# A hybrid decoder step on one core: rows spread by TensorE, attention work reordered, small work of the routing moved ahead of the weight splits

## The chip, the cores and the metric

One core of a Trainium2 chip runs the whole step in one launch. The metric is the device time of one execution in microseconds. TensorE (PE) multiplies, VectorE (DVE) and ScalarE (ACT) do elementwise work, GpSimd (POOL) small vector work and some DMA issues, SyncE (SP) issues the loads. TensorE runs at one of two clock levels, 1.2 or 2.4 GHz, and the profile shows which was granted (0.50 or 1.00).

## The reference, cut to what matters

336 tokens (8 sequences of 8 new tokens, 16 meta tokens and 256 prompt tokens; three tiles of 112 rows), D = 1024, go through two layers:

```
layer 0: x += pool(rmsnorm(x, g_mix)) ; pool: per 256-channel group, trailing mean minus token, @ pool_w[g], * pool_scale
         x += swiglu(rmsnorm(x, g_ffn))                                  # dense, D_FF = 2816
layer 1: proj = rmsnorm(x) @ w_in (1024 x 672) -> query latent 384, key/value latent 256, rotary key 32
         q = rmsnorm(cq) @ w_uq ; 16 heads of 64 + 32
         q_lat = q_nope @ w_uk ; scores = q_lat . ckv + q_pe . kpe ; softmax ; (p @ ckv) @ w_uv ; @ w_o
         prompt: 272 keys ; each sample sequence: 1024 cached keys + its own 8 new ones
         x += sum over the top 2 of 8 experts of gate * swiglu(rmsnorm(x))
y = rmsnorm(x)
```

All is float32. The kernel multiplies most of it as pairs of float32r parts: w = wh + wl, x = xh + xl, and three products.

## The kernel before

Each engine runs its own instruction list, joined by semaphores; the order within a list is written out by hand, and an engine never passes an instruction that waits.

**Head.** SP loads the tokens x, the gain g_mix and the scale of the pooling weights; both rows are broadcast by DMA, to 112 and 128 partitions (0.45 and 0.5 MB of writes). Per tile ACT squares (L740), POOL takes the inverse root (L629, L631), DVE multiplies (`norm`, L1054), ACT makes the high half (`tokens_split`, L753) and DVE the low half (L1081). ACT's list squares tile 1 before it makes the high half of tile 0. TensorE pools by multiplying with band matrices (L1590), with products of zeros in between (`add_zeros`, L1578; 40 at the start, 8 after a tile). POOL scales the pooling weights in two halves (L650), ACT and DVE split them (L763, L1092), and 72 matmuls make the pooling output (`three`, L1570 to L1572). DVE adds it, norms, and the dense loop starts at 52.36 us.

**Projection.** `project_in` makes the 672 columns in blocks of 512 and 160 with 24 matmuls each.

**Attention.** After the heads' queries are turned (L1756), TensorE makes all six blocks of values (L1768), then the queries absorbed into the latent space (L1778), then turns the cached keys of the first sequence (`turn_cache`, L1802), and waits for all six copies of these before the first prompt scores (`prompt_scores`, L1818 to L1823). The prompt loop is a pipeline over 20 units (4 groups of one `tail` and four `head` units): scores of u, turn of u-2 (`prompt_turn`, L1831), values of u-3 (`prompt_values`, L1840 to L1852). Then the eight sequences, one after another: scores against the cache (n = 0, 1) and the 8 new keys (n = 2: six matmuls and one for the rotary part), softmax, values (L1941), with the turns for the next sequence and pieces of the output projection (`fill`) in between. SP loads the pages of sequence b+3 once the output of sequence b is made (`load_cache`, one register load and two DMAs per page); POOL copies the rotary keys (L677) before TensorE may turn that sequence.

**Routing.** Three router tiles (L1964), a chain of small DVE operations, counts by TensorE (L1981, L1991), then POOL gathers the first item's tokens by an indirect DMA (L695), TensorE turns them (L1998), ACT and DVE split them, and the expert loop begins: 8 items of 33 weight units (1 MB each, ring of 11), each split by ACT (L732) and DVE (L1066) and used by 12 or more matmuls. The gate weights (`pick`, an Exp on ACT, L995) are made between the first splits. The first Silu (L983) and the first Exp (L919) each have a table load in front.

## Time and profile before

Three runs took 1425.63, 1427.50 and 1430.47 us (median 1427.5). The profiled execution took 1426.08 us, its span is 1424.5 us.

| stretch, us from the start | what | PE busy | granted clock |
|---|---|---|---|
| 0 to 52.4 | head: pooling layer | with gaps | 0.50 from 13.7 to 24.0 and 30.8 to 37.6, else 1.00 |
| 52.4 to 312.3 | dense SwiGLU | full | 1.00 but for 3.4 us |
| 312.3 to 358.9 | projections | 46.16 of 46.60 | 1.00 |
| 376.6 to 406.6 | values, absorbed queries, first turns | with gaps | 0.50 from 392.6 |
| 406.6 to 463.1 | prompt attention | nearly full | 0.50 to 423.3 and twice 3.4 us, else 1.00 |
| 463.1 to 591.3 | eight sequences | 125.6 of 128.3 | 1.00 |
| 591.3 to 639.9 | last projection, routing | with gaps | 0.50 from 617.9 |
| 639.9 to 1424.5 | experts | full but for 1.6 us at 666 and the end | 0.50 to 645.2 and from 669.1 to 672.5, else 1.00 nearly to the end |

How to read it: PE carries 86% of the chain that ended last. An instruction's line gives its start, its duration and, in brackets, how long its engine was idle before it and for whom it waited. PE durations overlap, so a matmul's pace is the distance between starts. SPq rows are DMA issues of SP.

### The profile page before, as it was taken

The numbers are of one execution on the slowest core, as the hardware profiler recorded it, in microseconds if no ns is written. First come the engines' busy times: TensorE is split into PE (matmuls) and PEld (weight loads), VectorE is DVE, ScalarE is ACT, GpSimd is POOL, SyncE is SP. The second block draws the span as 40 slices with busy tenths as digits, with TensorE's granted clock in tenths as the row PEclk, the third lists the DMA queues.
The fourth block names the chain that finished last, engine by engine and source line by source line (L and its number), as shares of the span: only waits on it lengthen the run. The fifth ranks groups of instructions, "written<-read, shape, count | busy, mean of one in ns | idle before, by whom it ended". The sixth has DMA issues, their size and how long they took to land.

```text
span 1424.5 us, 19477 instructions
## 1 busy us (share of the span) xinstructions
PE 1364.4 (96%) x6975; PEld 1122.2 (79%) x6975; DVE 955.5 (67%) x921; ACT 795.2 (56%) x786; POOL 96.7 (7%) x129
## 2 busy tenths in 40 slices
PE   7999999989989999959999999999999999999996
PEld 6899989877667777537888888888888888888884
DVE  4634344355345444347888888888888888888885
ACT  4423333334445333225777777777777777777773
POOL 3000000002200000110001001000010010100100
PEclk7999999999959999968999999999999999999998
DMA  9644443230210422377999999999999999999981
GB/s 265 222 152 135 130 147 118 84 132 12 64 40 1 157 70 59 137 308 270 367 362 365 401 364 369 388 361 390 369 366 400 364 369 387 362 389 370 362 322 37
DMA packets 137428, 355.04 MB, mean 249 GB/s; under 512 B 18426, under 2 KB 54858, under 8 KB 137377
## 3 DMA queue, kind: packets, MB, share of 16 engines
q1 hardware_dynamic: 133769, 342.37, 65.9%
q0 software_dynamic: 3616, 12.09, 2.9%
q8 instruction: 28, 0.46, 0.1%
q14 instruction: 15, 0.12, 0.0%
HBM read 345.38 MB, written 9.20 MB: 249 GB/s over the span
## 4 chain that ended last, share of the span: by engine, by line
PE 86%; SPq 4%; DVE 3%; issue 2%; ACT 2%; DMA 1%; POOL 0%; ACTq 0%; DVEq 0%; POOLq 0%
PE PS L1570 24%; PE PS L1572 24%; PE PS L1571 24%; PE PS L1872 2%; PE PS L2005 1%; SPq L556 1%; SPq L554 1%; SPq L552 1%; PE PS L1941 1%; PE PS L1768 1%; PE PS L1852 1%; DMA X<-in_x_prompt 1%; PE PS L1778 1%; PE PS L1998 1%; PE PS L1590 1%
## 5 line engine op out<-in xcount | busy, mean ns | idle before, releaser
L1066 DVE TENSOR_TENSOR LOW<-RAW,UH 128x2048 fp32r<-128x2048 f32 x275 | 628.3, 2292 | 152.4 <-ACT UH L732 152.4
L732 ACT CAST UH<-RAW 128x2048 fp32r<-128x2048 f32 x275 | 526.2, 1914 | 252.3 <-PE PS L1572 252.2
L1570 PE MATMUL PS<-UH,XH 128*128 128x512 f32 (+1 forms) x768 | 292.1, 380 | 1.4 <-DVE XL L1446 1.4
L1572 PE MATMUL PS<-UH,XL 128*128 128x512 f32 (+1 forms) x768 | 290.2, 378 | 0.0
L1571 PE MATMUL PS<-LOW,XH 128*128 128x512 f32 (+1 forms) x768 | 290.2, 378 | 0.0
L1570 PEld LDWEIGHTS PS<-UH,XH 128*128 128x128 f32 x768 | 145.7, 190 | 30.1 <-DVE XL L1446 1.8
L1572 PEld LDWEIGHTS PS<-UH,XL 128*128 128x128 f32 x768 | 145.3, 189 | 28.8
L1571 PEld LDWEIGHTS PS<-LOW,XH 128*128 128x128 f32 x768 | 145.5, 189 | 28.2
L1570 PE MATMUL PS<-UH,ATH 128*128 128x512 f32 x352 | 138.7, 394 | 1.9 <-DVE ATL L1462 1.9
L1572 PE MATMUL PS<-UH,ATL 128*128 128x512 f32 x352 | 137.9, 392 | 0.0
L1571 PE MATMUL PS<-LOW,ATH 128*128 128x512 f32 x352 | 137.7, 391 | 0.0
L1570 PE MATMUL PS<-HTH,UH 128*128 128x336 f32 x352 | 111.2, 316 | 0.6 <-DVE HTL L1073 0.6
L1571 PE MATMUL PS<-HTL,UH 128*128 128x336 f32 x352 | 110.9, 315 | 0.0
L1572 PE MATMUL PS<-HTH,LOWPAIR 128*128 128x336 f32 x352 | 110.8, 315 | 0.0
L1570 PEld LDWEIGHTS PS<-UH,ATH 128*128 128x128 f32 x352 | 66.5, 189 | 16.1 <-issue 2.3
L1572 PEld LDWEIGHTS PS<-UH,ATL 128*128 128x128 f32 x352 | 66.4, 189 | 14.1
L1571 PEld LDWEIGHTS PS<-LOW,ATH 128*128 128x128 f32 x352 | 66.5, 189 | 13.7
L1066 DVE TENSOR_TENSOR LOWPAIR<-PAIR,UH 128x2048 fp32r<-128x2048 f32 x22 | 50.4, 2293 | 27.9 <-ACT UH L732 27.9
L1570 PEld LDWEIGHTS PS<-HTH,UH 128*128 128x128 f32 x352 | 66.1, 188 | 1.5 <-issue 1.0
L1571 PEld LDWEIGHTS PS<-HTL,UH 128*128 128x128 f32 x352 | 66.2, 188 | 0.4
L1572 PEld LDWEIGHTS PS<-HTH,LOWPAIR 128*128 128x128 f32 x352 | 66.1, 188 | 0.0
L799 ACT CAST AH<-AF 128x336 fp32r<-128x336 f32 x22 | 10.4, 473 | 81.7 <-DVE AF L1144 81.7
(315 smaller groups left out, 1697.0 us busy)
## 6 DMA issues: line engine op xcount, KB each, us to landing
RAW<-in_moe_w_down SPq DMA_DIRECT2D x88, 1024.0 KB, 5.1
RAW<-in_moe_w_gate SPq DMA_DIRECT2D x64, 1024.0 KB, 5.1
RAW<-in_moe_w_up SPq DMA_DIRECT2D x64, 1024.0 KB, 5.0
RAW<-in_moe_w_gate SPq DMA_DIRECT2D x24, 768.0 KB, 7.3
RAW<-in_moe_w_up SPq DMA_DIRECT2D x24, 768.0 KB, 7.6
PAIR<-in_ffn_w_gate SPq DMA_DIRECT2D x11, 1024.0 KB, 5.3
PAIR<-in_ffn_w_up SPq DMA_DIRECT2D x11, 1024.0 KB, 7.8
RAW<-in_ffn_w_down SPq DMA_DIRECT2D x11, 1024.0 KB, 4.9
```

The lines of the kernel that those rows point to most:

```text
L552: page = sp.value_load(PAGES[0:1, b * NPG:(b + 1) * NPG][:, bass.ds(i, 1)], min_val=0, max_val=nphys - 1)
L554: sp.dma_start(CC[b % 3][:, to, 0:KL], a["cache_ckv"][0, one, :, :].rearrange("e p c -> p e c"))\
L556: sp.dma_start(CC[b % 3][:, to, KL:KL + ROPE], a["cache_kpe"][0, one, :, :].rearrange("e p c -> p e c"))\
L732: nc.scalar.copy(dst, src).then_inc(unit_high, 1)
L1066: V_.tensor_tensor(dst, src, high.bitcast(F32), ALU.subtract).then_inc(unit_low, 1)
L1570: mm(out, wh, xh, start=start, stop=False, skip_group_check=True)
L1571: mm(out, wh, xl, start=False, stop=False, skip_group_check=True)
L1572: return mm(out, wl, xh, start=False, stop=stop, skip_group_check=True)
L1590: return mm(PS[:, d, t * TT:t * TT + wide], part[:, t, d * P:(d + 1) * P], pm[min(t, 1)][:, d // 2, 0:wide], start=False, stop=False, skip ...
L1768: ins = mm(PS[0:rows, half, :], CKT[:, c, SMP + p0:SMP + p0 + rows], WUV[:, c, half * 512:(half + 1) * 512], start=(c == 0), stop=(c == 1))
L1778: ins = mm(PS[:, 2 + n, hh * SMP:(hh + 1) * SMP], UKT[:, h, c * P:(c + 1) * P], QTR[0:NOPE, h, 0:SMP], start=True, stop=True)
L1872: ins = mm(PS[0:TT, mix_bank(i), :], OT[:, k, t * TT:(t + 1) * TT], WO[:, k, half * 512:(half + 1) * 512], start=(k == 0), stop=(k == KD - 1))
```

## The change

Nothing of the computed result changes. Head: the two rows are loaded to one partition and multiplied by a row of ones; ACT copies g_mix and DVE pool_scale out of PSUM ahead of the rest. The number of zero products in front goes from 40 to 24, and ten wider ones stand before the pooling output. ACT's tile order changes, one half of the pooling weights is scaled by DVE, an output DMA goes later. The projection's blocks become 336 + 336. Absorbed queries and values alternate, values 4 and 5 go later, all sequences' new-key scores are made once at prompt unit 2, and the wait for the first sequence's turned keys moves behind the first scores. Exp and Silu get a small early use on ACT. In the routing `pick` and the Exp move ahead of splits, `keep_clock` adds 18 and 28 transposes whose output nobody reads, and the first Silu moves ahead of a split.

```diff
+        sp.dma_start(ROWS[:, 0, :], a["g_mix"][0:1, :]).then_inc(rows_in, 16)
+        sp.dma_start(ROWS[:, 1, :], a["pool_scale"][0:1, :]).then_inc(rows_in, 16)
-        sp.dma_start(G[0][:, :], a["g_mix"][0:1, :].partition_broadcast(TT)).then_inc(gain0_in, 16)
-        sp.dma_start(PSC[:, :], a["pool_scale"][0:1, :].partition_broadcast(P)).then_inc(pool_w_in, 16)
...
# POOL
-        pool.dma_start(o["pool_sample"][0, :, 0:BUF - NS, :], a["state_pool"][0, :, NS:BUF, :])...
-        for half in range(2):
+        pool.wait_ge(spread_out, 4)
+        weights, scale = scaled_half(1)
+        pool.wait_ge(pool_w_scaled, 1)
             nc.gpsimd.tensor_tensor(weights, weights, scale, ALU.mult).then_inc(pool_w_scaled, 1)
         pool.wait_ge(normed, NT)
...
+        pool.dma_start(o["pool_sample"][0, :, 0:BUF - NS, :], a["state_pool"][0, :, NS:BUF, :])...
# ACT
+        for h in range(2):
+            act.wait_ge(rows_spread, h + 1)
+            nc.scalar.copy(G[0][:, h * 512:(h + 1) * 512], PS[0:TT, h, :]).then_inc(spread_out, 1)
         square(0, 0, x_in[0], 16 * 3)
+        tokens_split(0)
         square(0, 1, x_in[1], 16)
-        tokens_split(0)
+        tokens_split(1)
         square(0, 2, x_in[2], 16)
-        tokens_split(1)
         tokens_split(2)
...
+        query_latents_high(0); rotary_copy(0); query_latents_high(1); rotary_copy(1); query_latents_high(2)
         nc.scalar.copy(NKH[:, :, :], CKT[:, :, 0:SMP]).then_inc(operand_high, 1)
+        query_latents_high(3)
+        nc.scalar.activation(SS[:, 24:26], NHALF[:, :], ACT.Exp)
...
         split_first(2)
-        tokens_high(0)
         act.wait_ge(r_dve, 1)
         nc.scalar.activation(RC[:, 6:8, :], RC[:, 4:6, :], ACT.Exp).then_inc(r_act, 1)
-        nc.scalar.copy(YS[:, 0:2], RPS[0][:, 0:2]).then_inc(i_y, 2)
+        nc.scalar.activation(YS[:, 0:2], RPS[0][:, 0:2], ACT.Silu).then_inc(i_y, 2)
+        tokens_high(0)
         for n in range(NF):
-            split_first(n + HIGH) if n + HIGH < NF else split(0, n + HIGH - NF)
             if n == NF - 2:
                 gate(0, NU + NF - 1)
+            split_first(n + HIGH) if n + HIGH < NF else split(0, n + HIGH - NF)
# DVE
+        for h in range(2):
+            dve.wait_ge(rows_spread, h + 3)
+            if h == 0: dve.wait_ge(spread_out, 2)
+            V_.tensor_copy(PSC[:, h * 512:(h + 1) * 512], PS[:, 2 + h, :]).then_inc(spread_out, 1)
...
+        weights, scale = scaled_half(0)
+        V_.tensor_tensor(weights, weights, scale, ALU.mult).then_inc(pool_w_scaled, 1)
...
+        for n in range(4):
+            query_latents_low(n)
+            values_out(n)
...
-            link(V_.tensor_tensor_reduce(DM[:, :], PS[:, 2, 0:NS], cn("maskd"), 1.0, LOW, ALU.add, ALU.max, DS[:, 0:1]))
+            link(V_.tensor_reduce(DS[:, 0:1], DM[:, b, :], AX.X, ALU.max))
...
+        pick(logits, RC[:, 10:12, :]) and its maximum and difference, then:
         low_first(0)
-        tokens_low(0)
         low_first(1)
+        tokens_low(0)
# PE
+        for n in range(4):
+            rows = TT if n < 2 else P
+            mm(PS[0:rows, n, :], ONES[:, 0:rows], ROWS[:, n // 2, n % 2 * 512:n % 2 * 512 + 512], start=True, stop=True)\
+              .then_inc(rows_spread, 1)
+        pe.wait_ge(spread_out, 4)
...
-        add_zeros(0, P, T, 32)
+        add_zeros(0, P, T, 16)
...
+        pe.wait_ge(pool_dve, 1)
+        for _ in range(10):
+            mm(PS[:, 0, :], ZB[:, 0:P], ZB[:, :], start=True, stop=True)
         for n, (t, half) in enumerate(POOL_ORDER):
...
-            lo, hi = ((0, 512), (512, PROJ))[block]
+            lo, hi = ((0, PROJ // 2), (PROJ // 2, PROJ))[block]
...
+        for n in range(4):
+            query_latents(n)
+            values(n)
         pe.wait_ge(ql_ev, 4)
+        for g in range(3): turn_cache(0, g)
+        values(4)
+        for g in range(3, 6): turn_cache(0, g)
-        pe.wait_ge(d_cte_dve, 6)          # now in prompt_turn(0)
+        def new_keys():
+            for b in range(NB):
+                here = slice(b * NS, (b + 1) * NS)
+                for c in range(2):
+                    three(PS[:, 7, here], QLH[:, c, b, :], QLL[c][:, b, :], NKH[:, c, here], NKL[:, c, here], c == 0, False)
+                ins = mm(PS[:, 7, here], QPS[:, b, :], NKR[:, here], start=False, stop=True, skip_group_check=True)
+            ins.then_inc(new_mm, 1)
...
             prompt_scores(u)
+            if u == 1: values(5)
+            elif u == 2: new_keys()
...
+        def keep_clock(count):
+            for _ in range(count):
+                nc.tensor.transpose(PS[:, 6, 0:P], ident, ident)
+        keep_clock(18)
         pe.wait_ge(diag_made, 2)
...
+        keep_clock(28)
         pe.wait_ge(i_idx, 1)
         turn_tokens(0)
```

## Rows read from the trace of the kernel before

**Rows 1.** Windows, head: stretch, us, busy per engine (instructions), PEclk, DMA share, GB/s
```profile
13.70:24.00 10.30, 8.70 (x39) 7.83 (x40) 6.59 (x6) 5.64 (x8) 3.94 (x6) 0.50 1.06 267
...
30.80:37.60 6.80, 5.54 (x26) 5.54 (x27) 6.03 (x7) 4.15 (x6) 0.00 (x0) 0.50 1.06 384
```

**Rows 2.** Timeline, head: start, us, engine, line, instruction, idle before and for whom
```profile
13.08 1.06 ACT L740 ACTIVATE SCR<-X 112x1024 f32<-112x1024 f32 x1 [5.23 <-DMA X<-in_x_prompt]
...
14.13 1.03 ACT L753 CAST HNH<-HN 112x1024 fp32r<-112x1024 f32 x1
...
24.33 5.19 POOL L650 TENSOR_TENSOR PW<-PW,PSC 128x1024 f32<-128x1024 f32 x2 [5.16 <-DMA PW<-in_pool_w]
...
32.06 0.55 PE L1570 MATMUL PS<-PWH,DTH 128*112 128x256 f32 x1 [2.19 <-DVE PWL L1092]
```

**Rows 3.** Timeline, projection: 24 matmuls of 160 columns, 24 of 512, the turn
```profile
318.63 0.31 PE L1570 MATMUL PS<-WINH,HTH 128*112 128x160 f32 x1
...
321.03 0.42 PE L1570 MATMUL PS<-WINH,HTH 128*112 128x512 f32 x1
...
326.59 0.93 PE L1563 MATMUL PS<-CN,HN 112*128 112x112 f32 x8
```

**Rows 4.** Windows, absorbed queries and prompt attention
```profile
387.00:392.60 5.60, 5.60 (x51) 5.53 (x50) 2.06 (x3) 1.17 (x2) 0.00 (x0) 1.00 0.23 61
...
411.15:423.30 12.15, 12.15 (x60) 9.02 (x61) 5.39 (x30) 4.62 (x19) 0.61 (x1) 0.50 0.07 19
```

**Rows 5.** Timeline, values to prompt attention
```profile
376.56 10.58 PE L1768 MATMUL PS<-WUV,CKT 128*128 128x512 f32 x24
...
397.42 2.82 PE L1802 MATMUL PS<-CN,CC 128*128 128x128 f32 x12 [1.45 <-DVE QLL L1259]
...
406.60 1.14 PE L1823 MATMUL PS<-KT,QTR 96*32 96x272 f32 x8 [1.39 <-DVE CTR L1276]
...
408.52 1.28 ACT L919 ACT_TABLE_LOAD   x1 [2.69 <-DVE RPS L1294]
...
411.15 0.90 PE L1831 MATMUL PS<-CN,PP 128*128 128x128 f32 x3 [0.55 <-DVE PP L1302]
...
417.34 0.80 PE L1818 MATMUL PS<-KT,QTR 96*128 96x128 f32 x2
...
421.03 1.14 PE L1823 MATMUL PS<-KT,QTR 96*32 96x272 f32 x8
...
425.89 0.49 PE L1818 MATMUL PS<-KT,QTR 96*128 96x128 f32 x2
...
428.07 0.49 PE L1818 MATMUL PS<-KT,QTR 96*128 96x128 f32 x2
```

**Rows 6.** Timeline, sequence 6: scores of the new keys, then the turn of sequence 7
```profile
561.86 0.25 PE L1571 MATMUL PS<-NKL,QLH 128*128 128x8 f32 x1
...
562.41 0.25 PE L1906 MATMUL PS<-NKR,QPS 96*128 96x8 f32 x1
562.72 1.09 PE L1802 MATMUL PS<-CN,CC 128*128 128x128 f32 x8
...
562.05 0.62 POOL L677 COPY CC<-CC 128x512 f32<-128x512 f32 x1 [15.81 <-DMA CC<-in_cache_kpe]
```

**Rows 7.** Routing and the first expert units: timeline, then windows
```profile
636.60 1.94 PE L1998 MATMUL PS<-CN,XN 128*128 128x128 f32 x8 [5.04 <-DMA XN<-tokens_normed,IDX]
...
617.90:636.60 18.70, 5.66 (x35) 5.16 (x32) 10.07 (x38) 5.78 (x4) 2.97 (x5) 0.50 0.80 306
...
639.90:645.20 5.30, 5.26 (x12) 4.13 (x13) 5.09 (x7) 0.07 (x1) 0.77 (x1) 0.50 0.28 99
```

**Rows 8.** First item's gate: timeline, then window
```profile
667.83 1.09 PE L2005 MATMUL PS<-CN,EA 128*128 128x128 f32 x8 [1.62 <-DVE EA L1455]
...
669.10:672.50 3.40, 3.40 (x10) 2.65 (x9) 2.02 (x4) 0.00 (x0) 0.18 (x1) 0.50 0.10 40
```

**Rows 9.** Window, expert loop
```profile
800.00:1000.00 200.00, 200.00 (x963) 166.62 (x961) 173.95 (x95) 147.97 (x98) 13.27 (x10) 1.00 1.00 378
```

More of the change, by code:

```diff
@@ L892, in cache_out, with query_latents_high @@
             nc.scalar.copy(keys_turned(CTH, CTR, b, g), PS[0:rows, turn_bank("cache", b, g), :]).then_inc(d_cte_act, 1)
-        for n in range(4):
+        def query_latents_high(n):
             c, g = n // 2, n % 2
@@ L1277, in cache_out @@
                              ALU.subtract).then_inc(d_cte_dve, 1)
-        for g in range(6):
+        for g in range(3):
+            cache_out(0, g)
+        values_out(4)
+        for g in range(3, 6):
             cache_out(0, g)
@@ L1758, in _, with query_latents @@
             ins.then_inc(qt_t, 1)
-        pe.wait_ge(wuv_in, 16)
-        for i, (p0, rows) in enumerate(KB):
-            for half in range(2):
-                n = 2 * i + half
-                if n >= 2:
-                    pe.wait_ge(v_ev, n - 1)
-                else:
-                    pe.wait_ge(qt_act if n else qt_dve, 5)
-                for c in range(2):
-                    ins = mm(PS[0:rows, half, :], CKT[:, c, SMP + p0:SMP + p0 + rows],
-                             WUV[:, c, half * 512:(half + 1) * 512], start=(c == 0), stop=(c == 1))
-                ins.then_inc(v_mm, 1)
         pe.wait_ge(qt_dve, H // 2)
         pe.wait_ge(qt_act, H // 2)
-        for n in range(4):
+        def query_latents(n):
             c, g = n // 2, n % 2
@@ L1836, in prompt_values @@
             pe.wait_ge(s_ptc, 2 * u + 2)
+            if kind == "tail" and n == 1:
+                pe.wait_ge(new_out, 1)
             if kind == "head":
@@ L1858, in _ @@
                 prompt_scores(u)
+            if u == 1:
+                values(5)
+            elif u == 2:
+                new_keys()
+            elif u == 3:
+                pe.wait_ge(v_ev, 6)
             if 2 <= u < NAU + 2:
@@ L1895, in _ @@
             pe.wait_ge(d_cte_dve, 6 * b + 6)
-            if b == 0:
-                pe.wait_ge(ql_ev, 7)
-            for n in range(3):
-                width = 512 if n < 2 else NS
-                if n == 2 and b >= 2:
-                    pe.wait_ge(d_olc, b - 1)
-                here = slice(n * 512, n * 512 + 512) if n < 2 else slice(b * NS, (b + 1) * NS)
-                high, low, rotary = (CTH[b % 2], CTL[b % 2], CTR[b % 2]) if n < 2 else (NKH, NKL, NKR)
+            for n in range(2):
+                here = slice(n * 512, n * 512 + 512)
                 for c in range(2):
-                    three(PS[:, n, 0:width], QLH[:, c, b, :], QLL[c][:, b, :], high[:, c, here], low[:, c, here], c == 0, False)
-                ins = mm(PS[:, n, 0:width], QPS[:, b, :], rotary[:, here], start=False, stop=True, skip_group_check=True)
+                    three(PS[:, n, :], QLH[:, c, b, :], QLL[c][:, b, :], CTH[b % 2][:, c, here], CTL[b % 2][:, c, here], c == 0, False)
+                ins = mm(PS[:, n, :], QPS[:, b, :], CTR[b % 2][:, here], start=False, stop=True, skip_group_check=True)
             ins.then_inc(d_s, 1)
@@ L2123, with value_bank @@
 MIX_UNITS = [b for b in range(1, NB - 1) for _ in range(4)] + [NB - 1] * 8
+def value_bank(n):
+    return (0, 1, 0, 1, 7, 6)[n]
 def mix_bank(i):
```

143 lines of the change are left out of this document (93 added, 50 removed).

## The prediction

> **What bounds the kernel now.** I read the profile in four steps. The page's chain of waits first: TensorE carries 86% of it, so the question in every stretch is whether TensorE gets its next instruction earlier or runs it at the higher clock. Then windows, stretch by stretch, for the granted clock; then the timeline around each place that the diff touches; last the expert loop, to see whether an earlier start of it reaches the end. There TensorE is busy 200.00 of 200.00 us at full clock [rows 9], and nothing in the loop changes, so what is gained in front of it shortens the run one for one. That loop is 55% of the time; everything below is about the rest.
>
> The time is lost in front in two ways. TensorE waits for other engines at the joints [rows 2, 5, 7, 8], and after stretches with little in them it stands at 1.2 GHz, where the same work takes up to twice as long [rows 1, 4, 7, 8].
>
> **Head.** Two broadcasts (about 0.95 MB of writes) leave a DMA system that is full (share 1.06) from 13.7 us on [rows 1], and the output DMA of 0.2 MB goes later. At the 267 GB/s of that window this is 1.15 MB / 267 = 4.3 us that the pooling weights and all later loads land earlier; the weights' arrival at 24.33 is what POOL waits 5.16 us for, and its two scalings then take 5.19 us [rows 2]. The second scaling now runs on POOL beside the first on DVE. ACT's copy for tile 0 was held to 14.13 behind the square that waited for tile 1's tokens at 13.08 [rows 2]; it now goes first. Against this stand new steps in front of tile 0: a float32 product of one row, two ACT copies for the gain, and two DVE copies of pool_scale ahead of the first norm. Tiles then follow each other on square, root, norm, copy, and the third tile's copy, not the first one's, gives the pooling its last operand. So I don't count the first tile's gain.
>
> What I count is the second low stretch. From 30.80 to 37.60 TensorE had 26 records in 5.54 busy us at 0.50 [rows 1], after it had waited 2.19 us for the split weights [rows 2]. The ten zero products fill that wait; at full clock the 5.54 us become 2.8. Added to that, the earlier weights could take off up to the 2.19 us of wait; against it, the first tile may start later than now. Lower end: the clock stays low and the 16 + 8 zero products after the spread delay the pooling, +2. Upper end: both low stretches go, (8.70 + 5.54) / 2 = 7.1 [rows 1], and the wait too, about 9. I take -3.0, near the one term that the rows carry, since the other has the third tile in its way. First_high, the adds and norms behind it keep their lengths.
>
> **Projection.** 24 matmuls of 160 columns take 321.03 - 318.63 = 2.40 us, 0.100 each; 24 of 512 take 5.56 us, 0.232 each [rows 3]. The short ones cost well over their columns' share (160/512 x 0.232 = 0.072). A 336-column one costs 0.152 by columns or 0.166 on the line through both. A tile now costs 7.96 us, then 48 x 0.152 = 7.3 or 48 x 0.166 = 7.97. TensorE is nearly gapless here, so the gain for three tiles is between 0 and 2.0; I take -1.8, because 336 columns are far from the size at which the short ones stop following their columns.
>
> **Absorbed queries, values, first turns.** Now all values take 376.56 to 387.1, six groups of 1.76 us, and the queries run 0.11 us per record (51 in 5.60) [rows 4, 5], 1.8 us per group of 16. TensorE then waits for the low half (1.45 us at 397.42), for copies that free its banks, and for the last of six copies until 406.60 [rows 5]. In the new order four queries and four values end near 377.2 + 4 x 1.8 + 4 x 1.76 = 391.4; the low halves run beside the values. Three turns (12 records at about 0.11, 1.3 us), values 4 (1.8) and three turns, which DVE's copies hold up by some 2 us, bring the first prompt scores to about 396.7: 9.9 us earlier. Nothing is queued behind the moved wait but prompt_turn(0), which comes later anyway.
>
> Before that turn the list now has values 5 (1.8 us) and the new keys: 8 x 7 matmuls at (562.41 - 561.86) / 5 = 0.11 us [rows 6], 6.2 us. With three units' scores (2.2) the turn starts at 406.9, against 411.15 [rows 5]: -4.3. DVE and ACT reach their part of it near 401, also because the table load of 1.28 us at 408.52 [rows 5] is now made ahead, so TensorE's own list is the bound and that saving is mostly hidden. The Trainium skill, page "ScalarE: Activation LUTs", section "What ACT_TABLE_LOAD costs", puts a switch of tables at 1.28 us and a drain of 1.38 us, about 2.7 together. The trace agrees with the first; by the page the two switches would be worth 2.8 us more than I count where they lie on the chain.
>
> Then the clock. It fell at 392.6, after 5.60 us in which TensorE had no gap but only 64-column products [rows 4], and stayed at 0.50 to 423.3. The mixture with 512-column values should keep it up through 400, but the 56 products of 8 columns are thinner than what preceded the fall. I expect it to fall during them and to return within about 10 us. A head unit takes 421.03 - 417.34 = 3.69 us at the low clock and 428.07 - 425.89 = 2.18 at the full one [rows 5]. Of the 12.15 low us after the first turn [rows 4] all saved would be worth 12.15 x (1 - 2.18/3.69) = 5.0 us; I take 2.0. Sum for the prompt part -6.3, between -1 (the clock and the joint go worse) and -12.
>
> The page "TensorE: Matmul & The Clock Gate" of the Trainium skill, section "HAM oscillation — how this bites in real kernels", ties the fall to idle gaps of TensorE while it waits. By that the gapless new keys would cost no clock. Rows 4 show a fall without a gap, so I hold to the rows.
>
> **The eight sequences.** The new keys leave each sequence's list: 7 x 0.11 = 0.77 us, 6.2 in all. But a second chain runs beside: SP loads pages one after another from the end of sequence 0 on. At sequence 7 POOL waited 15.81 us for the last page, copied to 562.67, and TensorE's turn began at 562.72, 0.2 us after its last new-key product could end [rows 6]. From 477.5 (first output made) to 562.72 the loads set the time. A shorter list there turns into TensorE waits. Only sequence 0 in front of it and sequence 7 behind it gain: 2 x 0.8 = -1.6, between 0 and -6.2.
>
> **Routing.** TensorE was busy 5.66 of 18.70 us and low from 617.9, and stayed low from 639.9 to 645.2 for the first 12 expert products [rows 7]. The added transposes fill the waits for DVE and for the gather (5.04 us at 636.60). If the clock is up by then, 12 products at 5.26 / 12 = 0.44 come down to the 0.23 of rows 3 and save 2.5 and the turn and splits of the tokens 0.4: -2.9. If it isn't, 28 transposes at about 0.21 us take 5.9, about 1 more than the wait of 5.04 and the turn starts later: +1. DVE makes the gate's picks (about 1 us) and two splits first, ready as the high half is. I take -2.9; the ends are +1 and -3.5.
>
> **First item.** TensorE waits 1.62 us at 667.83 for the gated product, behind a split and a table load on ACT, and its clock then falls for 3.40 us, 10 records [rows 8]. With the gate ahead of the split the product can be ready when TensorE has done the gate sums: -1.6, and the low stretch goes: -1.7. Between -1 and -3.5.
>
> **Sum.** -3.0 - 1.8 - 6.3 - 1.6 - 2.9 - 3.3 = -18.9. The profiled execution took 1426.1, so 1407.2 by its own time; the median of the runs shown is 1.4 higher: 1408.5.
>
> **Rivals.**
> The first is on the other side: the new keys pull the clock down at about 406 and the prompt loop, with its 16-column tails, never fills TensorE enough to get it back. For it: two more falls inside the loop, and 30 us at 0.50 before. Against it: it came back at 423.3 in the same loop. Price: the 33 us that ran at full clock after 423.3 take 3.69/2.18 = 1.69 times as long, +22.8, and my 2.0 are lost: 1408.5 + 24.8 = 1433. It makes the kernel slower once about 27 of the 33 us run low.
> The second: the clock does not fall at the new keys, as the page would have it. Then the other 3.0 of the 5.0 come too, and the later falls may go: 1408.5 - 5 = 1403.5.
> The third: the weight stream is the real bound of the experts. DMA share is 1.00 at 378 GB/s [rows 9]. The stream starts when the sequences end, so it moves with everything before, but the gains of routing and first item (6.2) would be given back: 1414.7. Against it: TensorE shows no gap in that window.
> The fourth: the head gains nothing or loses up to 2, because spread and copies hold tile 0: 1411.5 to 1413.5.
> The fifth: SP's page loop isn't binding (its 2 us per page can tighten): 4.6 more, 1404.
>
> **How the numbers follow.** Forecast 0.60 (own range 1403 to 1414), slow clock 0.04, clock stays up 0.12, stream 0.07, head 0.11, SP 0.06. The range 1399 to 1417 takes in the forecast, the two fast ones, head and stream. 0.3% is 4.3 us, about what a measurement can tell from no change. Faster 0.93; slower 0.04, all from the first rival; same 0.03, where that rival is met half-way or several ends meet.
>
> **What would show it.** Dense loop starting at 49 to 50 instead of 52.36; PEclk 1.00 in the pooling output; 24-matmul blocks of 336 taking 3.65 us; first prompt score near 394 and turn 0 near 404 on a clock shifted by head and projection (-4.8); POOL's page copies still 16 us apart with TensorE idle 0.6 to 0.8 us before each first turn; first expert products 0.23 us apart; no table load in front of the first gate. I am wrong if TensorE is low through most of the prompt loop, if the time between first and last page copy shrinks, or if gaps open in the expert loop.

## The result and the profile after

The changed kernel took 1421.29 us (median; 1418.27 to 1422.73), the kernel before in the same session 1427.68: a ratio of 0.9952, 95% interval 0.9931 to 0.9973. It is faster by 6.4 us. The forecast was 1408.5, its range 1399 to 1417: about a third of the forecast gain came. The profiled execution took 1418.27, its span is 1416.6 against 1424.5: 7.9 us less.

Stage by stage in the two profiled executions, between first starts of TensorE's groups, in us; the forecast is the term of the sum:

| stage | before | after | difference | forecast |
|---|---|---|---|---|
| head, to the first dense product | 52.36 | 49.06 | -3.3 | -3.0 |
| dense, to the first projection product | 259.98 | 258.89 | -1.1 | 0 |
| projections, to the first key product | 46.41 | 44.84 | -1.6 | -1.8 |
| to the first turn of the prompt loop | 52.40 | 53.06 | +0.7 | -4.3 |
| prompt loop, to the end of its last values | 51.97 | 51.48 | -0.5 | -2.0 |
| eight sequences, to the last output's turn | 129.25 | 127.07 | -2.2 | -1.6 |
| last projection and routing | 47.57 | 46.17 | -1.4 | -2.9 |
| first item, to the second gated product's turn | 63.57 | 63.45 | -0.1 | -3.3 |
| the rest of the experts | 720.99 | 722.61 | +1.6 | 0 |

The rows that answer to [rows 1]: windows of the kernel after, head (columns as there).

```profile
13.70:24.00 10.30, 10.30 (x75) 8.31 (x74) 6.49 (x6) 4.28 (x7) 2.60 (x6) 1.00 1.09 310
...
30.80:37.60 6.80, 6.80 (x60) 6.80 (x59) 6.27 (x7) 2.40 (x3) 0.00 (x0) 1.00 1.07 386
```

Both stretches ran at 1.00. The timeline of VectorE and GpSimd in the head answers to [rows 2]: VectorE now scales one half of the pooling weights and GpSimd the other. They don't run beside each other as the forecast had it, since GpSimd waits for VectorE's half (`pool_w_scaled`), but VectorE's takes 1.22 us for GpSimd's 2.86, and both are done at 28.42 instead of 29.52.

```profile
24.64 1.22 DVE L1132 TENSOR_TENSOR PW<-PW,PSC 128x1024 f32<-128x1024 f32 x1
...
26.04 2.38 POOL L659 TENSOR_TENSOR PW<-PW,PSC 128x1024 f32<-128x1024 f32 x1 [5.86 <-DVE PW L1132]
...
28.08 1.41 DVE L1122 TENSOR_TENSOR PWL<-PW,PWH 128x1024 fp32r<-128x1024 f32 x1 [0.22 <-ACT PWH L773]
```

Timeline of the kernel after from the first scores to the first turn; it answers to [rows 5]. The new keys' 56 products begin at 396.00.

```profile
392.16 0.67 PE L1899 MATMUL PS<-KT,QTR 96*32 96x272 f32 x8
...
396.00 0.36 PE L1622 MATMUL PS<-NKH,QLH 128*128 128x8 f32 x1
396.22 0.25 PE L1623 MATMUL PS<-NKL,QLH 128*128 128x8 f32 x1
396.33 0.25 PE L1624 MATMUL PS<-NKH,QLL 128*128 128x8 f32 x1
...
398.45 0.29 PE L1622 MATMUL PS<-NKH,QLH 128*128 128x8 f32 x1
398.59 0.36 PE L1623 MATMUL PS<-NKL,QLH 128*128 128x8 f32 x1
398.81 0.35 PE L1624 MATMUL PS<-NKH,QLL 128*128 128x8 f32 x1
...
405.64 0.35 PE L1888 MATMUL PS<-NKR,QPS 96*128 96x8 f32 x1
405.85 0.47 PE L1909 MATMUL PS<-CN,PP 128*128 128x128 f32 x1
```

The first scores come at 392.16 instead of 406.60. The pace of the new keys is 0.11 us to 398.45 and 0.21 from there. And the first turn waits for nothing but them. VectorE had made its operand, the first unit's 272 columns of probabilities, at 396.11; ScalarE had done its part of the next two units too by 398.59 and was then idle for 8.19 us.

```profile
395.75 0.36 DVE L1348 TENSOR_SCALAR PP<-PP,RPS 128x272 f32<-128x272 f32 x1
...
398.40 0.19 ACT L944 ACTIVATION_READ_ACCUMULATOR PP<-PP,RPS 128x1 f32 x1
406.79 0.37 ACT L952 COPY PPT<-PS 128x256 f32<-128x256 f32 x1 [8.19 <-PE PS L1909]
```

The windows from the fall on, which answer to [rows 4]:

```profile
398.50:415.60 17.10, 17.10 (x83) 15.29 (x83) 3.16 (x17) 2.83 (x12) 0.61 (x1) 0.50 0.11 31
415.60:425.80 10.20, 10.07 (x79) 7.63 (x79) 6.28 (x31) 5.55 (x22) 0.00 (x0) 1.00 0.00 1
```

In the sequences [rows 6], GpSimd's copy of the last page of sequence 7 and the turn behind it:

```profile
554.90 0.62 POOL L687 COPY CC<-CC 128x512 f32<-128x512 f32 x1 [15.72 <-DMA CC<-in_cache_kpe]
555.57 1.09 PE L1852 MATMUL PS<-CN,CC 128*128 128x128 f32 x8 [0.67 <-POOL CC L687]
```

From VectorE's output of sequence 0 to this copy before took 562.05 - 477.60 = 84.5 us and now takes 554.90 - 471.07 = 83.8: the pace of the pages is the old one, and TensorE's list is short enough now to wait for it, as forecast.

Routing, tokens and first gate, against [rows 7, 8]:

```profile
627.95 1.06 PE L2088 MATMUL PS<-CN,XN 128*128 128x128 f32 x8 [1.92 <-DMA XN<-tokens_normed,IDX]
...
630.58 0.77 PE L1622 MATMUL PS<-UH,XH 128*128 128x512 f32 x1 [1.56 <-DVE XL L1498]
631.14 0.63 PE L1623 MATMUL PS<-LOW,XH 128*128 128x512 f32 x1
...
652.96 3.83 ACT L742 CAST UH<-RAW 128x2048 fp32r<-128x2048 f32 x2
...
654.89 2.29 DVE L1092 TENSOR_TENSOR LOW<-RAW,UH 128x2048 fp32r<-128x2048 f32 x1 [1.36 <-ACT UH L742]
657.10 1.21 DVE L1507 TENSOR_TENSOR EA<-EG,PS 128x1024 f32<-128x1024 f32 x1
...
658.37 1.97 PE L2095 MATMUL PS<-CN,EA 128*128 128x128 f32 x8 [2.33 <-DVE EA L1507]
```

The tokens' turn now runs at full clock (8 in 1.06 us, before 1.94), but the first products that follow are again slow. And the gate: the wait that was to go is longer, 2.33 us for 1.62. The gate ran ahead of the split on ScalarE, but the high half of the next unit stood behind it (652.96), VectorE waited 1.36 us for that half, made its low half, and only then the gated product. The table load that stood in front of the gate before (1.28 us at 664.20) is gone, as forecast. Before, the Silu began at 665.49, right where that load ended, so these rows show no drain that the change could save besides.

### The profile page after: what moved, and what is told of

Its sections match the earlier page's. It is cut to its first block, busy times and chain, and to the rows that moved or that the text cites. A ratio compares the mean times of both kernels' runs of the same rounds, so it can differ in the third digit from the quotient of the medians.

```text
span 1416.6 us, 19585 instructions
## 1 busy us (share of the span) xinstructions
PE 1366.6 (96%) x7022; PEld 1120.7 (79%) x7023; DVE 958.4 (68%) x918; ACT 796.5 (56%) x789; POOL 95.6 (7%) x128
## 4 chain that ended last, share of the span: by engine, by line
PE 87%; SPq 4%; DVE 3%; issue 3%; ACT 2%; DMA 1%; POOL 0%; DVEq 0%; ACTq 0%; POOLq 0%
PE PS L1622 25%; PE PS L1623 24%; PE PS L1624 24%; PE PS L1958 2%; PE PS L2095 1%; SPq L565 1%; SPq L563 1%; SPq L567 1%; PE PS L2025 1%; PE PS L1932 1%; PE PS L1828 1%; PE PS L1864 1%; PE PS L1801 1%; PE PS L1630 1%; PE PS L1636 1%
```

## Experiments

All were timed against the kernel before in the same session (its medians in the sessions: 1427.85, 1427.92, 1427.25, 1427.40, 1428.83). Where no kernel is named, the edit is made in the changed kernel. Stage times are read as in the table above, from one profiled execution of each kernel.

**New keys back in the sequences.** The part "new keys' scores once for all" alone is undone; the table load, the orders and all else stay.

```
-            elif u == 2:
-                new_keys()
...
-            for n in range(2):
+            for n in range(3):      # n == 2: this sequence's 8 new keys, 7 products
```

> The changed kernel with one edit undone: the scores of the new keys are again made sequence by sequence (7 thin matmuls behind each sequence's two wide blocks) and not 56 at once at prompt unit 2. Everything else stays. Theory A (the 56 thin products in a row pull TensorE's clock down and cost about 10 us in front of the first turn of the prompt loop, which eats what the reordering of values, queries and turns had gained): the first turn of the prompt loop comes 8 to 10 us earlier than in the changed kernel (405.99), near 397, the clock is 1.00 through the first group or nearly, the loop ends 8 to 11 us earlier, and the eight sequences take 1 to 2 us longer (first and last sequence 0.8 each); total 6 to 9 us less than the changed kernel's 1421.3, so 1412 to 1415. Theory B (the low stretch comes from the interleaved values, turns and waits themselves): the clock still falls between 392 and 400, the first turn comes about 6 us earlier at best and the loop runs low as before; total 1417 to 1420.

Measured: 1411.93 us (ratio 0.9876, 0.9845 to 0.9908), 9.4 less than the changed kernel. The first turn comes 43.40 us after the first key product instead of 53.06; the sequences take 129.20 instead of 127.07. Timeline of this kernel at the first turn, and the prompt loop as one window:

```profile
397.02 0.49 PE L1890 MATMUL PS<-KT,QTR 96*128 96x128 f32 x2
397.34 0.60 PE L1891 MATMUL PS<-KT,QTR 96*128 96x256 f32 x2
397.77 0.53 PE L1905 MATMUL PS<-CN,PP 128*128 128x128 f32 x3
...
397.77:448.72 50.95, 49.20 (x334) 36.79 (x333) 29.57 (x146) 24.72 (x92) 0.63 (x1) 0.87 0.06 14
```

So in the profiles hoisting cost 9.7 us at the joint and gave 2.1 in the sequences. The low stretch did not stay away (401.1 to 408.0), but is 6.9 us long instead of 17.1. In this profile routing took 53.12 us, 7 more than after, with a low stretch of 20.5 us; the kernel's other runs took 1407.94 to 1413.49 against the profiled 1417.29, so this was not met in all.

**New keys in four portions inside the prompt loop.**

```
+            if 3 <= u < 7:
+                new_keys((2 * (u - 3), 2 * (u - 3) + 1))
```

> The changed kernel, but the new keys' scores are made two sequences at a time in prompt units 3 to 6, each pair between that unit's turn and values, and not all at unit 2. Same number of matmuls. Theory A (it is their standing in one row that pulls the clock down): the first turn comes near 397 instead of 405.99, the clock does not fall, or for 3.4 us at most in the first group, each pair costs 1.5 us, and the loop ends 3 to 6 us earlier than in the changed kernel; total 1415 to 1419. Theory C (thin products cost the clock wherever they stand): the low stretch comes in units 3 to 6 and the loop ends within 1 us of the changed kernel's.

Measured: 1424.99 us (0.9977, 0.9958 to 0.9996), 3.7 more than the changed kernel. Theory A is right on the first turn, which comes early (43.40), and wrong on clock and time. Theory C is right that the low stretch comes with the portions, and wrong on its price: the loop takes 67.32 us and ends 6.2 us later after the first key product than in the changed kernel. TensorE ran 27.3 us of it at the low clock, prompt work and new keys alike. This profile is the slowest of the kernel's ten runs (1429.18, the others 1421.55 to 1427.61), so the stretch was shorter or absent in some.

```profile
402.80:430.10 27.30, 27.30 (x129) 23.67 (x129) 6.24 (x32) 5.37 (x20) 0.61 (x1) 0.50 0.06 14
```

**Zero products of 336 columns between the new keys.** Placed behind each of the first seven sequences' new keys, in otherwise unused columns of the bank.

```
+                if b < NB - 1:
+                    for _ in range(2):
+                        mm(PS[:, 7, P:P + 336], ZB[:, 0:P], ZB[:, 0:336], start=True, stop=True)
```

> The changed kernel with two zero products of 336 columns (into columns that nobody reads) behind each of the first seven sequences' new keys, 14 in all, about 0.14 us each at full clock, 2.0 us of extra work. Theory A (gapless products of 8 columns lower the granted clock, and their 9.9 us is 56 products at a pace of 0.21 instead of 0.11): the fall moves behind the new keys or stays away, they and the zeros take about 8 us together, the first prompt turn comes 1 to 2 us earlier than 405.9, and the 17 us low stretch at 398.5 shortens. Rival F (the fall comes from the stretch in front of them, scores and copies with waits, or comes at that place whatever TensorE does): still a fall near 398.5, the 14 products cost 2 to 4 us more.

Measured: 1425.31 us (0.9982, 0.9963 to 1.0001), 4 more than the changed kernel, the upper end of Rival F. What Theory A expected of wide products did not come: the clock fell 3.8 us into the new keys (2.5 without the zeros) and stayed low longer (20.5 us).

```profile
397.42:401.20 3.78, 3.78 (x36) 3.62 (x34) 2.13 (x10) 1.59 (x8) 0.00 (x0) 1.00 0.25 72
401.20:408.96 7.76, 7.76 (x39) 7.25 (x38) 0.00 (x0) 0.00 (x0) 0.61 (x1) 0.50 0.18 47
408.96:421.70 12.74, 12.74 (x64) 9.61 (x65) 4.38 (x23) 4.13 (x15) 0.00 (x0) 0.50 0.01 3
```

Every profile of this study has a fall somewhere between 390 and 408, with the new keys there or not. What differs is the length of the stretch: 17.0 to 17.1 us in the eight profiles with the keys in one block at that place (20.5 with the zeros among them), 27.3 with four portions, 3.4 to 6.9 us in the six of the new order with the keys in the sequences. Two of these six have another low stretch before it, at 374 (below). So the keys lengthen the stretch; what makes the clock fall there stays open.

**Gated product first.** VectorE's gated product of the first item goes ahead of the low split of the unit before.

```
-            if n == NF - 1:
+            if n == NF - 2:
                 hidden(0, 1, NU + NF)
             low_first...
```

> The changed kernel with the gated product of the first item (DVE, EA) one place earlier in DVE's list, ahead of the low half of unit 9, as ACT has its Silu ahead of the high half of that unit. Theory: the first item's gain was lost because DVE's product stood behind a low half that the Silu itself had pushed back by 1 us; then TensorE's wait of 2.33 us goes to under 0.3 and, if the clock then stays up, the low stretch of 3.4 us behind it goes too: total 2 to 4 us less than the changed kernel. Rival: the wait only moves, to the weights of unit 9, or the clock falls anyway: 0 to 1 us less.

Measured: 1416.11 us (0.9920, 0.9891 to 0.9949), 5.2 less than the changed kernel. That is more than the 2 to 4 expected. The first item takes 59.85 us instead of 63.45. Timeline of VectorE and TensorE of this kernel:

```profile
654.64 1.22 DVE L1507 TENSOR_TENSOR EA<-EG,PS 128x1024 f32<-128x1024 f32 x1 [1.37 <-PE PS L1624]
655.77 2.28 DVE L1092 TENSOR_TENSOR LOW<-RAW,UH 128x2048 fp32r<-128x2048 f32 x1
655.91 0.76 PE L2095 MATMUL PS<-CN,EA 128*128 128x128 f32 x5
```

2.2 us come at the turn itself, 1.4 from the low stretch at 657.9 to 661.4, which is gone. That is the gain that the forecast had put down to ScalarE's order.

**No filling in routing**, both `keep_clock` calls taken out.

> The changed kernel without the 18 and 28 transposes whose output nobody reads. Theory: with them gone the clock stays low through the routing as before, the first expert matmuls run 0.43 us apart for about 5 us, and the small products and the turn cost 0.6 us more each: 1.5 to 3 us slower than the changed kernel (1423 to 1424). Rival: they bring nothing, since the clock falls again at the waits for the gather and the splits: within 0.5 us.

Measured: 1423.54 us (0.9963, 0.9946 to 0.9979), 2.3 more than the changed kernel. Routing takes 49.26 us instead of 46.17, and the first item 64.55 for 63.45: the low stretch is 615.2 to 642.5, without a break. The fillings raise the clock up to the tokens' turn, as forecast; what they don't reach are the first products behind it.

**More filling in routing.**

```
+        keep_clock(14)
         pe.wait_ge(diag_made, 1)
...
+        keep_clock(10, 4)
         pe.wait_ge(i_xl, 2)
```

> Two more fillings of waits in routing: 14 transposes in front of the wait for the routing's one-hots (2.96 us in e1) and 10, on another bank, in front of the wait for the tokens' low half (1.56 to 1.9 us). Theory A (TensorE's waits there are what lowers the granted clock): the low stretches at 610.2 to 620.4 and 630.6 to 634.0 shrink or go; 1.5 to 3 us less. Rival E (the clock falls for the 8- and 14-column products and the 512-column product stretch in front, or the fillings delay what they precede): within 1 us of the changed kernel, or longer.

Measured: 1419.37 us (0.9945, 0.9927 to 0.9964), 1.9 less than the changed kernel, with overlapping intervals. In the profile only 610.2 to 617.0 is low between the sequences and the second gate; it is the fastest of the six runs (1414.73, the others 1417.85 to 1421.60), so this too was not met in all. Routing is no shorter for it (46.12 us), since the gather's arrival ends it, but the first item takes 60.46 us for 63.45:

```profile
627.34 1.06 PE L2089 MATMUL PS<-CN,XN 128*128 128x128 f32 x8 [1.88 <-DMA XN<-tokens_normed,IDX]
628.24 1.25 PE L2065 MATMUL PS<-CN 128*128 128x128 f32 x10
629.97 0.50 PE L1622 MATMUL PS<-UH,XH 128*128 128x512 f32 x1 [0.47 <-DVE XL L1498]
630.30 0.40 PE L1623 MATMUL PS<-LOW,XH 128*128 128x512 f32 x1
```

**Page loop written out.**

```
-            with sp.Fori(0, NPG) as i:
-                page = sp.value_load(PAGES[...][:, bass.ds(i, 1)], ...)
+            for i in range(NPG):
+                page = sp.value_load(PAGES[0:1, b * NPG + i:b * NPG + i + 1], ...)
```

> SyncE's loop over a sequence's 8 pages is written out, so that destinations are constants and no branch stands between pages; the new keys stay in front of the prompt loop. Theory A (SyncE's pace of about 2 us a page bounds the eight sequences, 113.3 us in the changed kernel, and hides what the new keys' removal freed): TensorE's waits for GpSimd's page copies go, sequences take 107 to 110 us, 3 to 6 us less in all. Rival C (the pages are held by their landing or by when their buffer comes free, not by the issue): sequences stay at 113 us, run within 1 us of the changed kernel.

Measured: 1415.28 us (0.9919, 0.9900 to 0.9938), 6.0 less than the changed kernel. The sequences take 122.90 us for 127.07, and no wait of TensorE for a page copy is left; this copy stood at 554.90:

```profile
547.72 0.61 POOL L687 COPY CC<-CC 128x512 f32<-128x512 f32 x1 [15.63 <-DMA CC<-in_cache_kpe]
```

From the output of sequence 0 to it pass 77.0 us instead of 83.8, for the 40 pages of sequences 3 to 7. SyncE's issue of the pages did bound the sequences.

**The ten zero products taken out**, those ahead of the pooling output.

> The ten products of zeros in front of the pooling output are taken out. Theory A (they fill the wait for the split weights and so keep the granted clock at 1.00 there): a low stretch of 3.4 to 6.8 us appears between 28 and 38 us, the dense loop starts 1.5 to 3 us later than 49.06, and the run is 1.5 to 3 us longer. Rival D (what the head gained came from earlier weights and GpSimd's share of the scaling alone): the loop starts at 49.1 or a little earlier, no difference.

Measured: 1421.20 us (0.9951, 0.9932 to 0.9969), no difference. A low stretch did appear, 29.4 to 32.8, and cost the pooling output 1.4 us, but the first dense product starts at 49.02 (after: 49.06). Timeline of this kernel:

```profile
29.53 0.56 PE L1622 MATMUL PS<-PWH,DTH 128*112 128x256 f32 x1 [2.60 <-DVE PWL L1122]
...
34.40 2.11 DVE L1145 TENSOR_TENSOR X<-X,PS 112x512 f32<-112x512 f32 x3
36.93 0.69 DVE L1145 TENSOR_TENSOR X<-X,PS 112x512 f32<-112x512 f32 x1 [0.42 <-PE PS L1624]
40.02 1.40 DVE L1145 TENSOR_TENSOR X<-X,PS 112x512 f32<-112x512 f32 x2
...
49.02 0.41 PE L1622 MATMUL PS<-HTH,UH 128*128 128x336 f32 x1 [0.55 <-DVE HTL L1099]
```

VectorE's list of splits, adds and norms takes up the slower products with one wait of 0.42 us. Its second split of the pooling weights starts 2.5 us earlier in the changed kernel than before (31.08 for 33.58), its first norm behind the pooling 3.3 us (38.85 for 42.14). So 2.5 of the head's 3.3 us lie in front of the pooling output. The other 0.8 lie where VectorE before waited 0.77 us for ScalarE and 0.69 for TensorE at its low clock; more than that the clock under the pooling output can't be worth. (e6 doesn't settle this rest: it had 3.4 us low there, the kernel before 6.8.)

**Combinations.** New keys back and gated product first; then with the added fillings; then with the page loop written out too.

> Two edits on the changed kernel: the new keys' scores go back into each sequence, and VectorE's gated product of the first item goes ahead of the split of the last unit. Theory A (the new keys cost TensorE 9.5 us in front of the prompt loop and give back 1.4 us in the sequences; the gate's lateness is a separate 2.5 us): the gains add, first prompt turn at about 397.7 on the span of a run whose projection starts at 307.95, median near 1410, 10 to 12 us below the changed kernel. Rival B (both gains draw on the same slack or are given back later, as e1's 5.5 us in the routing stretch of its profiled run): median no lower than 1412, e1's own.

> New keys back in the sequences, the first item's gated product ahead of the split, and both added fillings of routing. Theory A (three separate costs): e8's median of 1411.8 less the 2 to 3.5 us of the fillings, about 1409. Rival B (the fillings only paid by where the clock's stretches happened to lie, or share the first gate's gain): 1411 to 1412, as e8.

> As e11_back_gate_keep, and SyncE's page loop written out. Theory A (with the new keys in the sequences TensorE bounds them itself: no wait for GpSimd's page copies stood in e1's sequences): within 1 us of e11. Rival C (page loading still sets part of them): 3 to 4 us less than e11.

Measured: 1411.81 (0.9890, 0.987 to 0.991), 1410.67 (0.9884, 0.9856 to 0.9912) and 1410.73 us (0.9888, 0.9859 to 0.9917). In the profiles the stages add: first item 59.88, 58.32 and 58.32 us, and 43.40 to the first turn in the first two. In the third that is 47.98: a low stretch stands at 374.0 to 384.3 that the other two don't have. In the medians the gains don't add, against e1's 1411.93, as the Rivals B of e8 and e11 have it.

Each run's granted clock is on record and tells why the medians can't settle it. From clock and span, e1's four runs stood at 1.2 GHz for 34, 42, 51 and 62 us and took 1407.94, 1410.37, 1413.49 and 1417.29 us. Over all kernels timed here a run with 1 us more of low clock took 0.36 us longer than the others of its kernel (a fit, so an estimate). e8's five runs had 55 us low on average, e1's 47; set to the same low time, e8 is about 3 us faster than e1, so the gated product's gain is there (estimate). e11 and e10 aren't faster than e8 by this either: for the added fillings, Rival B stands to within what these runs can tell.

For the page loop Theory A is right: sequences 129.02, 129.07 and 129.04 us. With the keys in the sequences TensorE bounds them itself.

**The kernel before once more.** All nine profiles of the changed kernel and its variants up to then showed the expert item at 95.09 us, where the forecast counted on no change.

> The kernel before, profiled once more on this chip, to see whether the expert loop's item takes 94.86 us in it (as in its first profile) or 95.09 (as in all nine profiles of the changed kernel and its variants). Theory G (the profile of before ran 0.2% faster as a whole): 95.09 here, so 1.7 us of the difference between the profiles isn't the change's. Rival H (the change slows the loop): 94.86 again.

Measured: 1425.94 us (1.0002, 0.9981 to 1.0023). Timelines: the second and the twenty-third gated product's turn, seven items apart, here and in the kernel after.

```profile
699.73 0.71 PE L2005 MATMUL PS<-CN,EA 128*128 128x128 f32 x5
...
1363.70 0.71 PE L2005 MATMUL PS<-CN,EA 128*128 128x128 f32 x5
```

```profile
694.03 0.71 PE L2095 MATMUL PS<-CN,EA 128*128 128x128 f32 x5
...
1359.68 0.71 PE L2095 MATMUL PS<-CN,EA 128*128 128x128 f32 x5
```

(1363.70 - 699.73) / 7 = 94.85 us, (1359.68 - 694.03) / 7 = 95.09. Rival H: the change slows a loop of which it touches no line. The distances of TensorE's starts show where. Among the products of 512 columns from 800 to 1300 us, the one from LOW x XH to the UH x XL behind it is 0.2325 us on average before and 0.2366 after; the one from UH x XH to LOW x XH stays, and the third is 0.0015 shorter. One thing in the diff reaches there: DM, 32 bytes a partition there, now lies over an older tile, so that everything allocated behind it, weights and tokens too, lies 32 bytes lower.

**Tiles shifted.** 32 unused bytes in the changed kernel where DM had stood (tiles back at their old places); 64; 32 in the kernel before.

```
+    top[0] += 32
     PAGES = place("PAGES", [1, NB * NPG], I32)
```

> The changed kernel with 32 unused bytes per partition ahead of PAGES, in the place that DM held in the kernel before, so that every tile from PAGES on lies at its old address again. Theory J (the 32 bytes by which the weight and token tiles moved down are what makes the product behind LOW x XH start 6 ns later, 0.237 instead of 0.231): item of 94.86 us and dense stretch of 244.24 us as in both profiles of the kernel before, 1.7 + 0.5 = 2.2 us less. Rival K (another property of the changed program, its instructions' places or its semaphores, does it): 95.09 and 244.76, no difference.

> The same with 64 bytes. Theory J with a grid of 64 bytes or more (only the place in the grid counts): 95.09 us an item, as without the bytes. Rival L (a neighbourhood with other tiles counts, or the sum of the shift): another figure, or 94.86.

> The kernel before with 32 unused bytes ahead of PAGES, so that its tiles from there on leave the places they had. Theory J with a grid of 64 bytes: item of 95.09 us and dense stretch of 244.76, 2.2 us longer than the kernel before. Rival K: 94.86, no difference.

The same two turns in these three kernels, in this order:

```profile
697.39 0.71 PE L2096 MATMUL PS<-CN,EA 128*128 128x128 f32 x5
...
1361.35 0.71 PE L2096 MATMUL PS<-CN,EA 128*128 128x128 f32 x5
```

```profile
694.64 0.71 PE L2096 MATMUL PS<-CN,EA 128*128 128x128 f32 x5
...
1360.48 0.71 PE L2096 MATMUL PS<-CN,EA 128*128 128x128 f32 x5
```

```profile
706.73 0.71 PE L2006 MATMUL PS<-CN,EA 128*128 128x128 f32 x5
...
1372.57 0.71 PE L2006 MATMUL PS<-CN,EA 128*128 128x128 f32 x5
```

| place of the tiles | kernel | item, us | first to last HTH x UH product of the dense loop, us | run, us |
|---|---|---|---|---|
| old | before, e9 | 94.86, 94.85 | 244.24, 244.24 | 1427.68, 1425.94 |
| old | e13 (32 bytes) | 94.85 | 244.25 | 1417.87 |
| 32 bytes lower | after | 95.09 | 244.76 | 1421.29 |
| 32 bytes higher | e14 (64 bytes) | 95.12 | 245.41 | 1419.02, one run |
| 32 bytes higher | e16 (before, 32 bytes) | 95.12 | 245.41 | 1430.75 |

Theory J is shown: the place alone decides, in either kernel, and Rival K falls. The grid of 64 bytes falls too, since 32 lower and 32 higher differ in the dense stretch (244.76, 245.41), slightly in the item, and in which products are slow: with the tiles 32 higher all three distances of a triple are 0.234 us, each 1 to 2 ns longer.

The price by the stages is 1.7 + 0.5 us one way and 1.9 + 1.2 the other. By the medians it is 3.4 us in the changed kernel (0.9924, 0.9903 to 0.9946, against 0.9952; the intervals overlap) and 3.3 in the one before (1.0022, 1.0006 to 1.0038, timed against the unpadded kernel in one session). Set to the same low time as above, e13 is 2.2 us faster than the changed kernel, which is what the stages give (estimate).

**The version that beats both.** e10's edits and the 32 bytes.

> All edits of e10_all (new keys back, gate first, fillings, page loop written out) with the 32 bytes. Theory J: item of 94.86 us, 2.2 us under e10's 1410.7, about 1408.5. Rival K: as e10.

Measured: 1406.49 us (1406.24 to 1410.35; 0.9848, 0.9826 to 0.9871): 21 us under the kernel before and 15 under the changed one. The item is 94.86 us. To the first turn it takes 51.22 us, with a low stretch from 373.7 to 390.7, as e10. The same without the written-out page loop is the last run:

> e11_back_gate_keep (new keys back, gated product first, added fillings, SyncE's page loop as it was) with the 32 bytes. Theory J (the tiles' places cost what they cost in the changed kernel, 2.2 us by the stages and 3.4 by the medians): 2 to 3.5 us less than e11, 1407 to 1408.5. Theory M (besides, the written-out page loop is what brings the low stretch at 374 of e10's and e15's profiles, 4.6 to 7.8 us before the first turn): also less than e15's 1406.5, 1401 to 1404, and no low stretch at 374. If M is false: 1406 to 1408.

Measured: 1408.54 us (1404.68 to 1413.46; 0.9856, 0.9833 to 0.9879), 2.1 less than e11, at the edge of the 1407 to 1408.5 of Theory J, the item 94.86 us. Of Theory M one half came out: no low stretch at 374, 43.41 us to the first turn. But the written-out loop alone doesn't bring that stretch, since e5 has the loop and not the stretch; it stood only in the two kernels with both the loop and the keys in the sequences. The other half didn't come out: the median isn't below e15's (the intervals overlap), and the profile has low stretches of 3.4 us at 41.6, 297.6 and 311.2 that e15's lacks. What decides where such stretches fall is open. In the sum, e15 and e17 can't be told apart.

## Why the prediction was wrong, step by step

- **Head (-3.0, measured -3.3): right size by luck, wrong reason.** The forecast gave it to the clock under the pooling output, with the earlier weights as an addition. e6 let the clock fall for 3.4 us and lost nothing. At least 2.5 of the 3.3 us come from VectorE's second split of the weights, which starts that much earlier. No run takes back the scaling on VectorE or the rows spread by TensorE, so which of them does it is argued. And the size hangs on the profile of before: in its second one (e9) the second split starts at 31.88 and the dense loop at 50.47 instead of 52.36. Against that profile the head gained 1.4 us.
- **Dense (0, measured -1.1).** The low stretch at 300.4 to 303.9 is absent from this profile (about -1.6), the shifted tiles cost 0.52. Such stretches of 3.4 us come and go at 296 to 315 from one profile to the next: in the kernels with the changed projection and the tiles 32 bytes lower, dense and projections together take 303.7 to 303.8 us with none of them, 305.3 with one, 306.7 to 306.9 with two. The profiled execution of after met none; its time, 1418.27, is the lowest of its five runs and its granted clock, 0.982, the highest (the others 0.976 to 0.979). That fits the profiles' 7.9 us against the medians' 6.4.
- **Projection (-1.8, measured -1.6).** Right. The 336-column products started 0.154 us apart (three in 0.463), near the lower end of the forecast's two prices. The dense loop of the kernel before runs 336 columns too, at 0.153 us; that row would have given the price.
- **First turn (-4.3, measured +0.7): the step that failed.** Without the new keys the first turn comes 9.0 us earlier than before (43.40 for 52.40). The forecast put it at 406.9 - 6.2 = 400.7 on the clock of before, and e1's is 371.92 + 30.22 = 402.1 (30.22 us after the first turn of the queries, which before stood at 371.92): 1.4 off, all of it in front of the first scores. But the 56 products were priced at 0.11 us each, 6.2, from [rows 6], a place at full clock, though the next paragraph expected the clock to fall during them. At the low clock they pace 0.21; they took 9.85 us (396.00 to 405.85), and the turn came 9.7 later than in e1. That TensorE's own list bounds the turn was right: the turn's operand was ready at 396.11, on the clock of before 402.1 for the 401 forecast. So every microsecond of the mispriced products stood in front of the turn. The 1.4 and the 3.5 explain the 5.0 missing. (The signs that the prediction named, first score near 394 and turn 0 near 404, don't follow from its sum either: 396.7 and 406.9 less 4.8 are 391.9 and 402.1. Measured were 392.16 and 405.85.)
- **Clock in the loop (-2.0, measured -0.5).** It returned at 415.6, 17 us after the fall instead of 10. The first rival's mechanism is real, at a fraction of its price; with four portions (e2) the median is 3.7 us above the changed kernel's.
- **Sequences (-1.6, measured -2.2).** Right, cause too: e5 shows SyncE's page loop as the bound. But this should have been set against the cost: where the list is not the bound, taking 6.2 us out of it buys 2. The hoist was paid on the path and credited off it. Even with the loop written out it gives 129.0 - 122.9 = 6.1 us (e10 less e5) for 9.7.
- **Routing (-2.9, measured -1.4).** The turn came up to full clock, the first products did not, since the 1.56 us wait for the low half stood behind the last filling and the clock was low again from 630.6 to 634.0. In the profile of e7, which filled that wait, the first item takes 3.0 us less: 1.6 in front of the first gate and 1.4 from the low stretch at 657.9, which is absent. e4 shows that the fillings in the change are worth 2.3 us by the medians.
- **First item (-3.3, measured -0.1): failed.** The gate was ordered ahead on ScalarE alone. The forecast did not follow what this holds up: the next unit's high half, and through it VectorE's low half, behind which the gated product stood. e3 moved that too and got 3.6 us.
- **Experts (0, measured +1.6): failed.** "Nothing in the loop changes" holds for the lines, not for the addresses. The third rival (the weight stream) isn't it: TensorE still shows no gap, and it is the distance of one product in three that grew, by 4 ns, with the clock at 1.00; e13 took this back with nothing but padding.

In routing, low stretches are shorter where TensorE's waits are filled: 27.3 us without the fillings (e4), 10.2 and 3.4 with them, 6.8 with more (e7). At the new keys the clock fell without such a wait: TensorE was busy 26.86 of the 27.12 us from 371.38 to the fall at 398.5, its longest gap 0.13 us, and in the four portions it ran 27.30 of 27.30 us busy at the low clock. The page "TensorE: Matmul & The Clock Gate" of the Trainium skill, section "HAM oscillation — how this bites in real kernels", ties the fall to idle gaps of TensorE. In routing the traces agree, at the new keys they do not.

Missing in all, by the profiles: 18.9 - 7.9 = 11.0 us. First turn 5.0, first item 3.2, experts 1.6, loop 1.5, routing 1.5, projections 0.2, against which dense, sequences and head gave 2.0 more than forecast. The early tables, the moved wait and the order of queries and values were not undone one by one; e1 shows them together, as 9.0 us less to the first turn.

## What to carry to other kernels

Before work is moved forward out of a loop, ask at both ends what bounds it there: it costs in full where it arrives on the path (at the clock that the place has, not the one where it was measured), and gives back only what its old place didn't hide. When an instruction is reordered on one engine, follow the one that it pushes back through every engine to the next product. And where a tile is moved or resized, compare the addresses behind it: keep them, with padding if need be, or measure the long loops anew.

## What was not expected of the hardware

- Tiles 32 bytes a partition off their old place, either way, cost 0.24 to 0.27 us of an item of 94.85 and 0.5 to 1.2 us of a dense stretch of 244.2, with the same instructions in the same order. Which operand's address does it wasn't tried.
- Without any gap TensorE stood at 1.2 GHz for 27.3 us on products of 8 to 272 columns (e2), and 14 zero products of 336 columns among the new keys neither held the clock nor brought it back (e12).
- A low stretch in the head of 3.4 us cost the pooling output 1.4 us and the kernel nothing (e6). One at 41 to 45 us, behind it, moved the first dense product by about 1 us (e4, e8, e11, e17: 49.94 to 50.13 for 49.06).
